# Sixteen unused bytes between the tiles of a weight ring and ahead of two activation tiles, in a two-block transformer step on one core

## The reference

```python
def conv_ffn(h, w_in, conv_w, conv_b, w_down):
    a = h @ w_in                                   # 1024 -> 2 * 2816
    a = causal_depthwise_conv(a, conv_w) + conv_b  # width 3
    up, gate = jnp.split(a, 2, axis=-1)
    return (jax.nn.silu(gate) * up) @ w_down

def first_block(x, ...):
    h = x
    for l in range(2):
        if l < 1: h = h + gmlp_mixer(rmsnorm(h, a_norm_g[l]), ...)
        else:     h = h + chunk_attention(rmsnorm(h, b_norm_g[j]), k, v, ...)
        h = h + conv_ffn(rmsnorm(h, f_norm_g[l]), ...)
    return rmsnorm(h, final_norm_g)

def second_block(x, p, ...):
    h = x
    for i in range(2):
        h = h + (sb_rwkv_mixer(...) if i % 2 == 0 else mla_mixer(...))
        h = h + conv_glu(rmsnorm_2(h, ffn_norm[i]), ...)
        e = rmsnorm_2(p[i] @ ple_w_proj[i], ple_norm[i])
        h = h + jax.nn.sigmoid(rmsnorm_2(h, ple_gate_norm[i]) @ ple_w_gate[i]) * e
    return rmsnorm_2(h, final_norm)
```

## Time and profile before

| | us |
|---|---|
| median of 2 runs (1323.04 to 1324.91) | 1323.97 |
| the profiled execution, its own time | 1323.27 |
| its span, first to last instruction | 1321.5 |
| TensorE, matmuls in flight | 1300.0 |
| TensorE, weight loads in flight | 1268.0 |
| DVE busy | 913.0 |
| ACT busy | 758.1 |
| POOL busy | 44.1 |

### The profile page before, as it was taken

One profiled execution on the slowest core, in us unless ns is written; L12 is line 12 of the kernel. 1 busy time (PEld: TensorE's weight loads), 2 busy tenths in 40 slices (PEclk: granted clock), 3 DMA queues, 4 the chain that ended last, 5 costly groups with the idle time before them and its releaser, 6 DMA issues.

```text
span 1321.5 us, 29315 instructions
## 1 busy us (share of the span) xinstructions
PE 1300.0 (98%) x12222; PEld 1268.0 (96%) x12222; DVE 913.0 (69%) x1297; ACT 758.1 (57%) x977; POOL 44.1 (3%) x37
## 2 busy tenths in 40 slices
PE   9999999999999999999999999999999999999997
PEld 8999999998899999999989899999999889999997
DVE  4789886488479876468746387666578779666556
ACT  6667665367657665357554166554476876554444
POOL 1010000010010000010000010000001001000000
PEclk9999999999999999999999999999999999999999
DMA  8455555545345555535401135555435335555520
GB/s 333 175 208 191 191 190 191 191 191 195 125 160 191 191 190 191 191 122 191 160 34 37 65 136 211 182 184 199 179 141 187 130 128 200 192 190 190 191 96 33
DMA packets 31981, 220.63 MB, mean 167 GB/s; under 512 B 3712, under 2 KB 3840, under 8 KB 6160
## 3 DMA queue, kind: packets, MB, share of 16 engines
q1 hardware_dynamic: 30672, 213.36, 44.7%
q0 software_dynamic: 784, 4.85, 1.1%
q10 hardware_dynamic: 432, 1.05, 0.2%
HBM read 218.20 MB, written 1.05 MB: 166 GB/s over the span
## 4 chain that ended last, share of the span: by engine, by line
PE 87%; DVE 8%; ACT 3%; issue 1%; DMA 1%; POOL 0%; SPq 0%; DVEq 0%; ACTq 0%; POOLq 0%
PE ps L1850 22%; PE ps L1851 21%; PE ps L1852 21%; PE ps L1861 17%; DVE w_lo L1102 2%; PE ps L1856 2%; PE ps L1857 2%; PE ps L1858 2%; ACT w_hi L503 1%; DVE xt L1154 1%; PE ps L2072 1%; DMA raw<-stream 1%; DVE xA L1164 1%; DVE xB L1164 0%; DVE xB L1126 0%
## 5 line engine op out<-in xcount | busy, mean ns | idle before, releaser
L1102 DVE TENSOR_TENSOR w_lo<-raw,w_hi 128x2048 fp32r<-128x2048 f32 x197 | 449.9, 2288 | 149.3 <-ACT w_hi L503 148.8
L503 ACT ACTIVATE w_hi<-raw 128x2048 fp32r<-128x2048 f32 x197 | 376.2, 1913 | 169.8 <-PE ps L1852 165.4
L1850 PE MATMUL ps<-xB,w_hi 128*128 128x256 f32 x1120 | 314.4, 281 | 1.7 <-DVE up_acc L1228 1.7
L1852 PE MATMUL ps<-xB,w_lo 128*128 128x256 f32 x1120 | 312.7, 279 | 0.0
L1851 PE MATMUL ps<-xB,w_hi 128*128 128x256 f32 x1120 | 312.6, 279 | 0.0
L1850 PEld LDWEIGHTS ps<-xB,w_hi 128*128 128x128 f32 x1120 | 210.5, 188 | 3.1 <-DVE up_acc L1228 1.9
L1850 PE MATMUL ps<-xA,w_hi 128*128 128x256 f32 x744 | 210.7, 283 | 0.5 <-DVE w_lo L1102 0.5
L1851 PEld LDWEIGHTS ps<-xB,w_hi 128*128 128x128 f32 x1120 | 210.5, 188 | 0.1
L1852 PEld LDWEIGHTS ps<-xB,w_lo 128*128 128x128 f32 x1120 | 210.5, 188 | 0.0
L1851 PE MATMUL ps<-xA,w_hi 128*128 128x256 f32 x744 | 207.7, 279 | 0.0
L1852 PE MATMUL ps<-xA,w_lo 128*128 128x256 f32 x744 | 207.6, 279 | 0.0
(11 more groups left out here) (295 smaller groups left out, 1909.3 us busy)
## 6 DMA issues: line engine op xcount, KB each, us to landing
raw<-stream SPq DMA_DIRECT2D x199, 1024.0 KB, 4.8
raw<-stream SPq DMA_DIRECT2D x4, 512.0 KB, 7.6
at_bias<-rel POOLq DMA_DIRECT2D x1, 2048.0 KB, 8.1
hT<-x_t SPq DMA_DIRECT2D x4, 256.0 KB, 7.0
lora_w<-lora POOLq DMA_DIRECT2D x1, 1024.0 KB, 5.1
out_t<-xt SPq DMA_DIRECT2D x4, 256.0 KB, 2.4
hcon<-hyc POOLq DMA_DIRECT2D x1, 576.0 KB, 4.0
wsT<-wst ACTq DMA_DIRECT2D x1, 512.0 KB, 4.4
```

The costliest lines, as they stand in the source:

```text
L503: nc.scalar.activation(w_hi[c.slot][:], raw[c.slot][:], ACT.Copy).then_inc(hi_made, 1)
L1102: nc.vector.tensor_tensor(w_lo[c.slot][:], raw[c.slot][:], w_hi[c.slot][:].bitcast(F32), ALU.subtract).then_inc(lo_made, 1)
L1850: nc.tensor.matmul(out, wh, xh, start=start, stop=False, skip_group_check=True)
L1852: return nc.tensor.matmul(out, wl, xh, start=False, stop=stop, skip_group_check=True)
```

## The change

After each of the eight tiles `w_hi0..3` and `w_lo0..3` a tensor of four float32 (16 bytes) is taken that nothing uses. Another is taken between `xt` and `xA`, and a third kind ahead of `hid`, inside its `with` block. No instruction is added, removed or moved: on all five engines the instructions, their order, shapes and waits are the same ones, only line numbers and start bytes differ.

```diff
         raw = [sb(f"raw{i}", [P, CHUNK]) for i in range(RING)]
-        w_hi = [sb(f"w_hi{i}", [P, CHUNK], F32R) for i in range(RING)]
-        w_lo = [sb(f"w_lo{i}", [P, CHUNK], F32R) for i in range(RING)]
+        def stepped(name):
+
+            tiles = []
+            for i in range(RING):
+                tiles.append(sb(f"{name}{i}", [P, CHUNK], F32R))
+                sb(f"{name}_gap{i}", [P, 4])
+            return tiles
+
+        w_hi, w_lo = stepped("w_hi"), stepped("w_lo")
...
             xt = sb("xt", [P, KD, T], where=ph)
+            sb("xA_gap", [P, 4], where=ph)
             xA = sb("xA", [P, KD, 2, T], F32R, ph)
...
             with ExitStack() as f:
+                sb("hid_gap", [P, 4], where=f)
                 hid = sb("hid", [P, KF, 2, T], F32R, f)
```

## The result

The changed kernel takes 1335.26 us (median of two runs, 1335.25 and 1335.26) against 1323.97 us: a ratio of 1.0083, 95% interval 1.0066 to 1.0099. It is 11.3 us slower, small by the 2% measure but well outside the spread of the runs, and above the top of the range, 1332. The profiled execution took 1335.26 us, 11.99 more than the one of before.

What follows compares the result with a forecast made beforehand. TensorE's matmul pace was taken to bound the kernel: 1116 us, 84% of the span. The profiled 1323.27 us plus 0 + 0 + 0, with the runs' median 0.7 us higher, gave 1324.0 us; range 1319 to 1332.

Steps and rivals of the forecast that it cites:

- What bounds the kernel: TensorE's start-to-start pace: 9048 matmuls at 116.7 ns and 504 role-swapped at 118.3 ns, 1116 us, 84% of the span.
- Instructions, splits and transfers at 0: Nothing added or moved; ACT's copies, DVE's subtractions and small-tile loads at new start bytes: each taken as 0 us.
- TensorE's price for a start byte: Cost of ring matmuls reading operands at other places over 64: bounded from -23.5 to +7.5 us, taken as 0.
- All other blocks move by multiples of 64: Beyond the odd-slot ring blocks (4704 matmuls) and `xA` (2952), operands were claimed to keep their place over 64.
- the swapped form's 1.6 ns: With operand roles swapped, matmuls took 118.3 against 116.7 ns; explained by which operand is which, without any address.
- the steady pace of 116.7 ns: Ring matmuls before the change, 48 per 5.60 us whatever DVE and ACT do; taken as support for no address effect.
- the group's period of three: Operands of a group of three matmuls change at each step; claimed not to show in the starts, supporting 0 cost.
- C: Faster: TensorE's weight and moving reads stop disturbing each other where they stand alike; -23.5 us, 1300.5 us; chance 0.05.
- B: Slower: stationary or moving read dearer at its other place over 64; +7.5 us (1331.5) or +4.7 (1328.7); chance 0.09.
- D: Slower through DVE: odd slots' subtractions slow enough to be waited for; at worst 7.4 us, 1331 us; chance 0.02.
- the change isn't what it says: Allocator rounding leaves no tile at a 16- or 8-byte place; claimed time the same, within the no-effect case's 0.84.
- The sign that the prediction named: Profile check: 48 down-projection matmuls again 5.60 us in all slots; alternating chunks mean ring place, differing stages mean x place.

Runs made afterwards that it cites:

- Alone: Separate program computing nothing of the reference: only a ring block's three matmuls, ACT, DVE and transfers idle, at 128 pairs of distances; 113.3 to 126.7 ns a matmul.
- fast version: Against the kernel before: one gap of 128 bytes between `w_hi3` and `w_lo0`, one of 32 ahead of `xB`; 1298.77 us, ratio 0.9816.
- map: Against the kernel before: ring ordered hi0, lo0, hi1, lo1, 32 bytes ahead of each slot but the first, 128 ahead of `xA` and `hid`; 1334.86 us.
- the unrounded one: Against the kernel before: ring tiles 16 bytes apart over 64, `xA` 16 and `hid` 32 bytes beyond `xB`, by slices of wider tensors; 1342.01 us, ratio 1.0127.

## Why the prediction was wrong

**What bounds the kernel** was read rightly: the pace of the ring matmuls, 84% of the span by the prediction's sum and 83% by count (1096.3 of 1321.5 us). "A change of 1 ns in the pace is worth 9 us" held: the mean pace rose by 1.55 ns (116.81 to 118.36), by that 14.5 us, and 15.3 were counted.

**Instructions, splits and transfers at 0** held: DVE's and ACT's medians moved by 4 and 3 ns, and the transfers into `at_bias` and `hcon` took 8.0 and 4.1 us (8.1 and 4.0 before). `wsT` and `vnat`, both moved from 32 to 0, kept their 111 ns, as they kept their distance.

**The step that failed is TensorE's price for a start byte, taken at 0.** It was +15.3 us. Four things were wrong in it.

- It asked for the place of each operand over 64. The runs show that this place is worth nothing (everything moved together: 0.9996) and the distance between the two is worth up to 13 ns a matmul. "All other blocks move by multiples of 64" passed over chunks whose distance changed all the same, such as those of slots 0 and 2 under `xB` and `hid`; the stages under `xB` and `hid`, whose x tiles kept their place over 64, are most of the cost.
- It explained the swapped form's 1.6 ns by the roles. That row was a stream at a distance of 32 bytes instead of 224, so that the trace did have rows at two distances. Alone and not swapped, 32 bytes takes the same 118.3 ns, and with the x gaps alone the swapped form, its roles as before, fell to 113.3. The distance thus moves this form's pace; that it explains all of the 1.6 ns is not shown, since at 168 bytes the two forms differ (120.0 and 113.3).
- It took the steady pace of 116.7 ns to show that addresses do not matter. The ring's tiles lie whole multiples of 256 bytes from each other, and so do the x tiles, so that with weights stationary the trace held one distance, 224, again and again. A steady number over one value says nothing of the others.
- It said that neither the group's period of three nor the blocks' of six shows in the starts, and took them for even. Stretches of 48 matmuls are alike, but single steps are not: in the chunk of the earlier trace rows they go 120, 114, 116, 117 ns and again, with a period of four. The fast version's are 113 and 114. So the 116.7 ns was the mean of steps that something stretches, and the trace of before showed it.

**The rivals.** C had the mechanism, that the two reads of TensorE disturb each other by how far apart they stand, and the wrong sign and size for these distances: it argued that equal places free the reads, and at 0 / 128 bytes the pace is 119.1, at 0 / 0 (map and alone) 120.0. The objection to it, that reads at different rates don't keep their distance, did not keep the starting distance from mattering. C had 0.05, and B, with the right sign and too low a price for too few matmuls, 0.09 and 1331.5 us; both, and with them the range, were bounded by rows that could not carry it, and the 11.3 us lie beyond B's 7.5. D did not happen. That the change isn't what it says (steps of 32 bytes for gaps of 16) was true of the layout, and made it some 6 us cheaper than the unrounded one (1.0083 against 1.0127), not neutral.

**The page on the two read ports** (the Trainium skill, TensorE: Matmul & The Clock Gate, Step-by-step) says that loading the next weights doesn't take read bandwidth from the running matmul. Here the measurement decides: with TensorE alone at work the pace goes from 113.3 to 126.7 ns with nothing but start bytes changed. The prediction's estimate of 109.2 ns, from the same page's gap for a matmul by itself, was not reached at any of the 128 pairs.

**The sign that the prediction named** showed the effect, but had no reading for it: "if chunks alternate between two lengths, it is the place of the ring block", and if stages differ, the place of x. Both happened. Chunks alternate between four lengths, and the pairs of distances shift by one slot with each x tile, which is what a distance does and a place does not.

## What to carry to other kernels

In a kernel that TensorE bounds with one weight load to each matmul, look at the start-to-start pace and not only at waits: where it is steady and above its best, the start addresses of stationary and moving tiles are a knob, worth 7.6% here between best and worst (1397.3 against 1298.8 us), that costs no instruction. Find the distance by itself in a small program first, then try it in the kernel, since a stream can have more than one pace. And a row that is the same everywhere is no evidence that a quantity doesn't matter, if that quantity never varied.

## What the runs showed of the hardware

- With 128x128 float32r stationary blocks and 256 moving columns at the 2.4 GHz level, the mean pace depends on (stationary start minus moving start) over 256 bytes, of both stationary tiles, in steps as fine as the 4 and 8 bytes tried. Alone it lies between 113.3 and 126.7 ns, most often at 117.8 or 120.0 (51 of 128 pairs). 113.3 is the lowest steady pace seen.
- A slow pace is made of uneven steps that repeat: 120, 114, 116, 117 at 224 / 224 bytes, 118, 127, 135 at 148 / 20. At 64 / 192 the steps are 113 and 114.
- DVE, ACT and the transfers are not needed for it: most of the pairs tried both ways have the same pace in the kernels (DVE 68% and ACT 57% busy) and with both idle.
- Some distances have two paces or more (224 / 224: 116.7, 117.8 and 120.0 in one program; 88 / 88: 113.3 and 116.7 in one program; 64 / 64: 113.3 and 117.8 in the map). What chooses stays open, and so does why the pattern has a period of 256 bytes.
